# One vector instruction for both heads: the running sum and the high-half subtraction of prompt attention

## The reference

```python
z = jnp.einsum('bqhd,bkhd->bhqk', qb, kb) * scale + bias
mask = kpos[None, :] < qpos[:, None]
log_beta = jax.nn.log_sigmoid(z)
log_keep = jnp.where(mask, log_beta - z, 0.0)
rest = lax.cumsum(log_keep, axis=3, reverse=True) - log_keep
a = jnp.where(mask, jnp.exp(log_beta + rest), 0.0)
outs.append(jnp.einsum('bhqk,bkhd->bqhd', a, vb))
```

## Time and profile before

| what | before |
|---|---|
| device time, median of 3 runs | 3626.75 us (3626.16 to 3627.1) |
| profiled execution | 3627.95 us, span 3626.2 us |
| the block of prompt attention | about 2217 to 2604 us of the span |
| one pair of heads, all 12 tiles and the turn | 48.0 us |

### The profile page before, as it was taken

One profiled execution on the slowest core, in us unless ns is written; L12 is line 12 of the kernel. 1 busy time (PEld: TensorE's weight loads), 2 busy tenths in 40 slices (PEclk: granted clock), 3 DMA queues, 4 the chain that ended last, 5 costly groups with the idle time before them and its releaser, 6 DMA issues. The chain is left out here.

```text
span 3626.2 us, 56133 instructions
## 1 busy us (share of the span) xinstructions
PE 3166.2 (87%) x20656; PEld 2672.9 (74%) x20656; DVE 1961.4 (54%) x3395; ACT 923.5 (25%) x1598; POOL 445.2 (12%) x248
## 2 busy tenths in 40 slices
PE   5664999999995997799899997888794999999997
PEld 1234999999994997765565654444493999999995
DVE  2566555555555112266666666888615555555554
ACT  0114000000003002144444445777504000000003
POOL 0002111212210111100000000000010221222210
PEclk8887999999997998899999998999997999999998
DMA  8711111111100221399999993000001111111101
GB/s 329 254 48 58 41 35 46 38 43 46 40 23 29 80 78 52 127 380 404 395 397 398 397 408 103 24 24 18 24 23 29 47 41 46 46 46 46 46 23 49
DMA packets 215691, 433.75 MB, mean 120 GB/s; under 512 B 13664, under 2 KB 130057, under 8 KB 212441
## 3 DMA queue, kind: packets, MB, share of 16 engines
q1 hardware_dynamic: 215521, 431.67, 32.8%
HBM read 417.92 MB, written 13.92 MB: 119 GB/s over the span
## 5 line engine op out<-in xcount | busy, mean ns | idle before, releaser
L84 PE MATMUL bank<-hi,mlp_uphi 128*128 128x364 f32 (+1 forms) x1536 | 506.5, 330 | 92.5 <-POOL mlp_uplo L692 92.5
L85 PE MATMUL bank<-lo,mlp_uphi 128*128 128x364 f32 (+1 forms) x1536 | 506.6, 330 | 0.0
L86 PE MATMUL bank<-hi,mlp_uplo 128*128 128x364 f32 (+1 forms) x1536 | 506.4, 330 | 0.0
L85 PE MATMUL bank<-mlp_flo,mlp_dnhi 128*128 128x364 f32 (+1 forms) x1536 | 504.8, 329 | 0.0
L84 PE MATMUL bank<-mlp_fhi,mlp_dnhi 128*128 128x364 f32 (+1 forms) x1536 | 504.7, 329 | 0.0
L86 PE MATMUL bank<-mlp_fhi,mlp_dnlo 128*128 128x364 f32 (+1 forms) x1536 | 504.7, 329 | 0.0
L302 DVE SCALAR_TENSOR_TENSOR x_t<-bank,mod,x_t 128x364 f32<-128x364 f32 (+1 forms) x432 | 245.6, 571 | 379.0 <-PE bank L86 376.7
L84 PEld LDWEIGHTS bank<-hi,mlp_uphi 128*128 128x128 f32 x1536 | 290.4, 189 | 93.6 <-POOL mlp_uplo L692 93.6
L1291 PE MATMUL bank<-ident,sa_kraw 128*128 128x128 f32 x2048 | 278.7, 281 | 58.5 <-DMA sa_kraw<-in_cache_k 53.5
L1291 PEld LDWEIGHTS bank<-ident,sa_kraw 128*128 128x128 f32 x2048 | 225.8, 142 | 111.2 <-DMA sa_kraw<-in_cache_k 83.0
L1173 DVE COPY sa_kt<-bank 128x512 f32<-128x512 f32 x256 | 177.0, 692 | 215.6 <-PE bank L1291 211.7
(11 more groups left out here) (258 smaller groups left out, 5439.7 us busy)
## 6 DMA issues: line engine op xcount, KB each, us to landing
sa_kraw<-in_cache_k SPq DMA_DIRECT2D x256, 512.0 KB, 10.6
sa_vpage<-in_cache_v SPq DMA_DIRECT2D x256, 512.0 KB, 9.4
mlp_raw<-in_w_up SPq DMA_DIRECT2D x64, 512.0 KB, 4.0
mlp_raw<-in_w_down SPq DMA_DIRECT2D x64, 512.0 KB, 3.5
w_raw<-in_w_ada SPq DMA_DIRECT2D x24, 1024.0 KB, 8.6
pm_wada<-in_w_ada SPq DMA_DIRECT2D x48, 512.0 KB, 5.2
kv_raw<-in_w_kv SPq DMA_DIRECT2D x8, 1024.0 KB, 5.7
x_rows<-in_x_prompt SPq DMA_DIRECT2D x1, 4096.0 KB, 13.9
```

Source lines behind the costliest of these rows:

```text
L84: pe.matmul(out, w_hi, x_hi, start=start, stop=False, skip_group_check=True)
L85: pe.matmul(out, w_hi, x_lo, start=False, stop=False, skip_group_check=True)
L86: return pe.matmul(out, w_lo, x_hi, start=False, stop=stop, skip_group_check=True)
```

## The change

Both heads of a tile now share one DVE instruction for the running sum and one for the subtraction. The cast of head 0, the high half of head 1 on ACT, the clamps, and the matmuls stay as they are. `c_done` and `lo_done` now count once a tile and not twice. The core of the diff:

```diff
@@ POOL, clear @@
-                    pool.wait_ge(lo_done, 2 * last.n + 2)
+                    pool.wait_ge(lo_done, last.n + 1)
@@ ACT, exponential and high_half @@
-                    act.wait_ge(c_done, 2 * (x.n - 2) + h + 1)
+                    act.wait_ge(c_done, x.n - 1)
-                act.wait_ge(c_done, 2 * x.n + h + 1)
+                act.wait_ge(c_done, x.n + 1)
@@ DVE @@
-                    for h in range(2):
-                        c = c_run[:, x.h % 2, h, x.lo:512]
-                        dve.wait_ge(l_done, 2 * x.n + h + 1)
-                        if x.first:
-                            dve.wait_ge(zeroed, x.h + 1)
-                        else:
-                            dve.wait_ge(lo_done, 2 * (x.n - 1) + h + 1)
-                        dve.tensor_tensor(c, c, t[:, x.n % 2, h, 0:x.w], ALU.add).then_inc(c_done, 1)
-                    dve.wait_ge(c_done, 2 * x.n + 1)
+                    c = c_run[:, x.h % 2, :, x.lo:512]
+                    dve.wait_ge(l_done, 2 * x.n + 2)
+                    if x.first:
+                        dve.wait_ge(zeroed, x.h + 1)
+                    else:
+                        dve.wait_ge(lo_done, x.n)
+                    dve.tensor_tensor(c, c, t[:, x.n % 2, :, 0:x.w], ALU.add).then_inc(c_done, 1)
+                    dve.wait_ge(c_done, x.n + 1)
                     if x.n >= 2:
                         dve.wait_ge(tri_done, 2 * (x.n - 2) + 1)
                     dve.tensor_copy(c_hi[:, x.n % 3, 0, x.lo:512], c_run[:, x.h % 2, 0, x.lo:512]).then_inc(hi_done, 1)
-                    for h in range(2):
-                        dve.wait_ge((hi_done, hi_by_act)[h], x.n + 1)
-                        dve.tensor_tensor(c_lo[:, x.n % 3, h, x.lo:512], c_run[:, x.h % 2, h, x.lo:512],
-                                          c_hi[:, x.n % 3, h, x.lo:512].bitcast(F32), ALU.subtract).then_inc(lo_done, 1)
+                    dve.wait_ge(hi_done, x.n + 1)
+                    dve.wait_ge(hi_by_act, x.n + 1)
+                    dve.tensor_tensor(c_lo[:, x.n % 3, :, x.lo:512], c_run[:, x.h % 2, :, x.lo:512],
+                                      c_hi[:, x.n % 3, :, x.lo:512].bitcast(F32), ALU.subtract).then_inc(lo_done, 1)
@@ PE, tri @@
-                        pe.wait_ge(lo_done, 2 * x.n + h + 1)
+                        pe.wait_ge(lo_done, x.n + 1)
```

## The result

The kernel with the change takes 3731.4 us (median of 4 runs, 3728.47 to 3733.49), the kernel before 3626.45 us (3625.12 to 3627.1). The ratio is 1.0289, with a 95% interval of 1.0271 to 1.0307: 105 us slower. The forecast was 3689, with a range to 3715. The direction was right and the size was not: 62 us forecast, 105 measured.

What follows compares the result with a forecast made beforehand. The prediction took a loop through DVE, PE and ACT, closed by the merged subtraction, as the bound. Twelve tile steps sum to 55.9 us a pair against 48.0; eight pairs lose 63, less about 1: 3689 us, range 3665 to 3715.

Steps and rivals of the forecast that it cites:

- What bounds the kernel: Before the change no engine alone (DVE 41.5, PE 39.6, ACT 37.5 of 48 us); PE, ACT and DVE wait in turn.
- The loop: Subtraction, tri, ACT's weight to high half, next subtraction: 4.41 us, closed by the 1.22 merged subtraction into 5.63; chance 0.80.
- The length of a merged instruction: On DVE, one add or subtraction of 1024 columns takes about 1.22 us, saving 0.06 to 0.07 per merge.
- The add: Merged running-sum add on DVE: delays neither ACT's high half nor head 0's cast, and gains 0.06 us where DVE binds.
- The sum for a pair at the upper clock: Steps of the twelve tiles of a pair added up: 55.9 us against 48.0 before, a loss of 7.9 a pair.
- The clock: PE's granted clock: no term in the central sum; a few dips put only at the top of the loop's range, 3715.
- the loop's own range: Times allowed if the loop holds as worked out: 3668 to 3715 us, the top for a few clock dips.
- the twelve entries: One per tile of a pair, from the end of one merged subtraction to the next: 3.31 to 8.44 us.
- TensorE's clock falls: Rival: half of the tri lags run at 1.2 GHz, each doubled, adding 42 us in eight pairs: 3731; chance 0.07.
- The signs of the profile: Expected in the changed trace: full-tile subtraction waits of 0.9 to 1.2 us, DVE busy about 12 less, pair 56.
- DVE is the bound: Rival: DVE's saved 12.5 us all shows, since head 0's early start is worth nothing: 3614; chance 0.05.
- it only costs where a wait shows: Rival: only the 31 subtractions that waited for ACT pay 0.53 us each, loss 16.4, gain 12.5: 3631; chance 0.05.

Runs made afterwards that it cites:

- The two single-sided kernels: Kernel before, one wait changed each: tri of head 0 waits for both subtractions, 3685.23 us; head 0's subtraction waits for ACT's head 1 high half, 3686.51 us.

## Why the prediction was wrong, point by point

- **What bounds the kernel: right.** The loop read in the earlier trace rows is the loop that the changed kernel shows in its three waits. The two single-sided kernels confirm it.
- **The length of a merged instruction: right.** 1225 and 1216 ns against 1.22 us. (DVE's own step was added up as 4.45; its terms make 4.42, and nothing hangs on it.)
- **The add, "nothing is later here": wrong, and small.** The cast starts 0.04 to 0.05 us later, counted from the first add's start. The kernel with the merged add alone gained nothing and measured 5 us slower, of which its trace accounts for 1.5 in the length of the pairs.
- **The sum for a pair at the upper clock: right, 0.5 us short.** The sum had 55.9 us, and the one pair that ran at the upper clock throughout, in the kernel with repeated scores, took 56.4. It is not a lucky total: of the twelve entries each is within 0.15 us of its measured step (5.71 for n9 and n10, 5.01 for n11, 8.51 for n8, 4.10 for n0, 3.90 for n4, 3.25 for n1 and n5, 4.39 for n2 and n6, 3.87 for n7, 4.31 for n3). The gap between the high half and the subtraction, 0.10 and not 0.03, explains most of the 0.5.
- **The clock: this is the step that failed.** The central sum has no term for it. The text gave the clock a place only at the top of the loop's own range, "a clock that dips in a few places", by way of idle gaps of PE of up to 3 us at the turn. The loop at the upper clock makes 8 x 8.4 = 67 us of the block's 108, which leaves 41. In the trace of the changed kernel, what the steps take beyond their length at the upper clock adds up to 40 us: some 10 in the steps that end at n10, 8 at n3, 7 each at n4 and n11, 4 at n9, 3 at n7, and 2 at the other six. The repeated scores give 26 of it back; in their trace such steps still cost 12.
- **The rival's 3731: the right event, and luck in the digits.** "TensorE's clock falls" came to 3731 with 42 us for the clock, and 3731.4 was measured. But it had half of all tri lags slow and each doubled, at the turn and in the narrow tiles too. In fact 37 of 96 full tri matmuls were slow and the steps that begin with tri of 128 or 256 columns lost almost nothing, while a slow lag in a full tile was 2.11 for 1.22, not doubled, and cost 1.4 in the step, since the second weight came later as well. The clock row, 0.86 in the block, stayed above the 0.8 that was to be its sign.
- **Why 0.07 was too little.** The idle gap was forecast as 1.3 us in full steps and taken to be harmless. In the changed kernel, the clock fell with idle gaps of 1.72 us before tri of n9 and 2.57 before n8. The two events were also counted as rivals, though the second follows from the first: a longer loop idles PE, a slower PE makes the loop longer. With a longer loop at 0.80, the clock should have been a term of its sum.
- **The signs of the profile: mostly as told.** The subtraction's waits in full tiles are 1.57 us at the upper clock, not 0.9 to 1.2, and DVE is busy 9 us less in the block, not 12.
- **"DVE is the bound", and "it only costs where a wait shows": both fell,** by 105 us, and by the two kernels with single instructions at 3685 and 3687.

## What to carry to other kernels

Before two instructions of an engine are merged, ask of each who waits for the first alone, and whether that one leads back to what the second needs. If it does, the merge closes a loop whose length adds up the whole instruction and the whole way round, however idle the engines are; here a saving of 0.06 us bought a loop 1.2 us longer. And where the way round contains TensorE, a longer loop must be priced at both levels of its clock: the idle time that it makes can lower it.

## What the runs showed of the hardware

- PE fell to the lower clock in a stretch where it idled for at most 2.6 us at a time: idle gaps of 2.57 and 1.72 us before two tri groups, and granted 0.50 in the second. No gap of PE in the whole block of the changed kernel is longer than 2.6 us, and the granted clock from 2240 to 2590 was 0.86; in the kernel before the longest is 1.7, and the clock there was 0.98. The Trainium skill, in TensorE: Matmul & The Clock Gate, section Why this matters for your kernels, asks for no idle gaps of over about 3 us. Here keeping to that was not enough, and the measurement decides.
- Redundant matmuls in idle time raised the granted clock from 0.86 to 0.96 and made the kernel 26 us faster. In a kernel whose clock was at 0.98 the same ones cost 5 us, though the clock rose to 1.00.
- A DVE instruction that waited for two semaphores started 0.10 us after its releaser's end, one that waited for one 0.03 us after.
- Single DVE instructions of which the second does not need the first overlap by about 0.08 us in the records; one that needs its predecessor starts 0.03 after its end. So the saving of a merge can be lost at the next instruction. The Trainium skill's rule in Perfetto Trace Analysis, section Optimizing Scalar/DVE Operations, on grouping, held in size for the instruction itself (about 60 ns there; 1225 ns here for two that took 1.29 us). Its own condition, a saturated engine, was not met: DVE was busy 87% of the block's middle, and with the merged add alone no tile became shorter by more than 0.02 us.
